# Attention two heads at a time on one core: both key halves of the array in one pair of steps

## The reference, cut to what matters

```python
s = jnp.einsum('bqkgd,bskd->bkgqs', qblk, k).astype(jnp.float32) * scale
pr = jax.nn.softmax(s, axis=-1).astype(v.dtype)
return jnp.einsum('bkgqs,bskd->bqkgd', pr, v)
```

## Time and profile before

| | us |
|---|---|
| median of 3 runs | 3143.61 |
| lowest and highest | 3140.13, 3146.26 |
| the profiled execution | 3126.22 |
| its span | 3124.4 |
| TensorE, VectorE, GpSimd, ScalarE busy | 2777.1, 2225.4, 1640.1, 574.6 |
| attention of group 0, first scores to next matmul | 128.86 to 154.22 |
| attention of group 1 | 299.00 to 372.4 |
| attention of group 2 | 892.65 to 1061.45 |

### The profile page before, as it was taken

The page is one execution under the profiler, slowest core; times in us unless marked ns, Lnnn a source line. Parts: engine busy times, 40 slices in busy tenths (PEclk is TensorE's granted clock), DMA queues, the critical chain, the costliest instruction groups (busy, mean ns, idle before and its releaser), DMA issues.

```text
span 3124.4 us, 34577 instructions
## 1 busy us (share of the span) xinstructions
PE 2777.1 (89%) x9441; PEld 1620.8 (52%) x9441; DVE 2225.4 (71%) x4681; ACT 574.6 (18%) x983; POOL 1640.1 (52%) x1444
## 2 busy tenths in 40 slices
PE   7999998795258876967999999999999999999997
PEld 6785565465134435533366555555555545545553
DVE  1336567999988777899988677777777766655554
ACT  2311502210024200111166311111011111100001
POOL 0001354346577677456832466666666656655451
PEclk9999999898666788988999999999999999999999
DMA  4375698778789899777877899999999999998984
GB/s 148 108 236 176 181 340 285 265 274 299 246 300 310 302 372 370 251 236 249 276 268 270 325 401 403 401 401 399 390 397 389 378 372 401 401 347 323 327 318 167
DMA packets 360703, 961.16 MB, mean 308 GB/s; under 512 B 28065, under 2 KB 152737, under 8 KB 359073
## 3 DMA queue, kind: packets, MB, share of 16 engines
q0 software_dynamic: 184320, 671.17, 58.8%
q1 hardware_dynamic: 175136, 284.69, 26.3%
q10 hardware_dynamic: 1152, 4.19, 0.3%
HBM read 930.58 MB, written 29.36 MB: 307 GB/s over the span
## 4 chain that ended last, share of the span: by engine, by line
PE 67%; DVE 16%; DMA 6%; issue 4%; ACT 4%; POOL 2%; POOLq 0%; ACTq 0%; SPq 0%; DVEq 0%
PE o_bank L766 21%; PE bank L776 21%; PE bank L541 10%; DVE ring L1103 8%; PE bank L712 5%; PE bank L529 5%; DMA ring<-in_expert_u,idx_now 3%; POOL ring L1070 2%; PE o_bank L747 2%; PE bank L519 1%; PE o_bank L621 1%; PE bank L611 1%; DMA wslot<-in_expert_uT 1%; DMA ring<-in_expert_v,idx_now 1%; ACT region_p L970 1%
## 5 line engine op out<-in xcount | busy, mean ns | idle before, releaser
L1070 POOL DMA_INDIRECT ring<-in_expert_u,idx_now x640 | 784.5, 1226 | 461.4 <-DVE dots L1103 230.4
L1070 POOL DMA_INDIRECT ring<-in_expert_v,idx_now x640 | 750.7, 1173 | 467.0 <-issue 148.2
L766 PE MATMUL o_bank<-region_b,wslot 128*128 128x384 f32 x2048 | 687.8, 490 | 13.1 <-DMA wslot<-in_expert_uT 13.1
L776 PE MATMUL bank<-wslot,region_q 128*128 128x512 f32 x1536 | 679.9, 592 | 0.0
L1103 DVE CUSTOM_DVE_ANT_0 ring<-ring,h 128x1024 f32<-128x1024 f32 x512 | 606.2, 1220 | 63.4 <-DMA ring<-in_expert_u,idx_now 55.4
L1411 DVE SCALAR_TENSOR_TENSOR region_c<-ring,dots,region_c 128x1024 f32<-128x1024 f32 x384 | 492.9, 1284 | 105.5 <-DMA ring<-in_expert_v,idx_now 69.7
L766 PEld LDWEIGHTS o_bank<-region_b,wslot 128*128 128x128 f32 x2048 | 392.0, 192 | 315.8 <-issue 64.8
L776 PEld LDWEIGHTS bank<-wslot,region_q 128*128 128x128 f32 x1536 | 291.8, 190 | 340.3 <-issue 306.6
L1062 POOL COPY idx_now<-idx 128x8 uint32 x160 | 104.7, 654 | 509.5 <-DVE idx L1340 293.5
L712 PE MATMUL bank<-ring,region_s 128*128 128x512 f32 x512 | 246.7, 610 | 59.2 <-ACT region_s L948 49.2
L990 ACT ACTIVATE region_q<-o_bank 128x384 f32<-128x384 f32 x128 | 62.9, 491 | 980.6 <-PE o_bank L766 980.6
(11 more groups left out here) (158 smaller groups left out, 2529.3 us busy)
## 6 DMA issues: line engine op xcount, KB each, us to landing
wslot<-in_expert_uT SPq DMA_DIRECT2D x128, 512.0 KB, 11.8
wslot<-in_expert_v SPq DMA_DIRECT2D x128, 512.0 KB, 6.8
wslot<-in_w_in SPq DMA_DIRECT2D x34, 1024.0 KB, 7.0
wslot<-in_w_query SPq DMA_DIRECT2D x24, 1024.0 KB, 8.0
region_p<-expert_weights SPq DMA_DIRECT2D x20, 768.0 KB, 14.9
wslot<-in_w_out SPq DMA_DIRECT2D x12, 1024.0 KB, 11.6
expert_weights<-region_q SPq DMA_DIRECT2D x6, 2048.0 KB, 7.4
expert_weights<-region_p SPq DMA_DIRECT2D x6, 2048.0 KB, 7.4
```

What stands on the lines that cost most here:

```text
L766: ins = nc.tensor.matmul(dense_in[q][:, 0:DENSE_T], u_cols[slot][:, k, :], h2T[:, k, T - DENSE_T:T], start=(k == 0), stop=(k == KD - 1))
L776: ins = nc.tensor.matmul(dense_out[2 * t + n][:], hidden[q][:, t * P:(t + 1) * P], v_cols[slot][:, n * 512:(n + 1) * 512], start=start, st ...
L1070: nc.gpsimd.indirect_dma_start(ring[:, r, :], None, table, bass.IndirectOffsetOnAxis(ap=idx_now[:, half, r:r + 1], axis=0)).then_inc(row_l ...
```

## The change

Steps are taken in pairs (m is steps 2m and 2m+1, the two halves of the same j). TensorE issues both score matmuls of a pair one after the other, turns both steps, and interleaves the value matmuls of the two halves. `probs`, `neg_max` and `prob_sum` get four buffers; the transposes go to four half tiles in `gate_attn` and `keys_sb`, which attention did not use before. VectorE and ScalarE take maxima, exponentials, scalings and copies two at a time. No instruction is added or taken away.

```diff
--- before.py
+++ after.py
@@ -137,12 +137,15 @@
                 yield (gg, "qT", j), None
         yield (g, "kT"), None
     n = len(attention_steps(g))
-    yield (g, "s", 0), None
-    yield (g, "s", 1), None
-    for i in range(n):
+    for i in range(0, n, 2):
+        if i == 0:
+            yield (g, "s", 0), None
+            yield (g, "s", 1), None
         if i + 2 < n:
             yield (g, "s", i + 2), None
+            yield (g, "s", i + 3), None
         yield (g, "probsT", i), None
+        yield (g, "probsT", i + 1), None
     for c in range(KD // 2):
         for d in (2 * c, 2 * c + 1):
             yield (g, "gate_attn", d), (g, "gate_attn", c)
@@ -243,8 +246,8 @@
         dots_now = sb("dots_now", [P, BODY])
         stat = sb("stat", [P, 3, TT])
         head_stat = sb("head_stat", [P, TT, QK_HEADS])
-        neg_max = sb("neg_max", [P, 2])
-        prob_sum = sb("prob_sum", [P, 2])
+        neg_max = sb("neg_max", [P, 4])
+        prob_sum = sb("prob_sum", [P, 4])
         eps = sb("eps", [P, 1])
 
         xa = region_b[:, :].rearrange("p (t d) -> p t d", t=TT)
@@ -278,8 +281,14 @@
         mixedTs = [h2[:, 2:4, :].rearrange("p a d -> p (a d)").rearrange("p (g t) -> p g t", g=GROUPS),
                    region_s[:, 0:GROUPS * T].rearrange("p (g t) -> p g t", g=GROUPS)]
         kTs = [late[:, sizes[1]:sizes[1] + T], region_s[:, 0:T]]
-        probs = region_s[:, T:3 * T].rearrange("p (a s) -> p a s", a=2)
-        probsT = region_s[:, 3 * T:5 * T].rearrange("p (a s) -> p a s", a=2)
+        probs = region_s[:, T:5 * T].rearrange("p (a s) -> p a s", a=4)
+        turned_probs = [gate_attn[:, :, :].rearrange("p a t -> p (a t)"),
+                        keys_sb[:, :, :].rearrange("p a n -> p (a n)")]
+
+        def probsT(i):
+
+            return turned_probs[i // 2 % 2][:, i % 2 * T:(i % 2 + 1) * T]
+
         peer_q = region_s[:, 0:2 * T].rearrange("p (a t) -> p a t", a=2)
         score = region_s[:, 2 * T:6 * T].rearrange("p (a t n) -> p a t n", a=4, t=TT)
 
@@ -600,41 +609,44 @@
                 steps = attention_steps(g)
                 t0 = GROUP_OF[g][1][0]
 
-                def scores(i):
-                    t, j, half = steps[i]
-                    if i == 0:
+                def scores(m):
+                    t, j, _ = steps[2 * m]
+                    if m == 0:
                         moved(pe, FIRST_GROUP[b], "kT")
                         for jj in range(PAIRS):
                             moved(pe, g, "qT", jj)
-                    bank = fill(g, "s", i)
-                    rows = slice(half * HD, (half + 1) * HD)
-                    ins = nc.tensor.matmul(bank[:], qTs[g][rows, j, (t - t0) * P:(t - t0 + 1) * P],
-                                           kTs[b][rows, :], start=True, stop=True)
-                    done(ins, g, "s", i)
-
-                def values(i):
-                    t, j, half = steps[i]
-                    if j == 0 and half == 0 and b * TT + t >= 2:
+                    pair = [fill(g, "s", 2 * m + half) for half in range(KV_HEADS)]
+                    for half in range(KV_HEADS):
+                        rows = slice(half * HD, (half + 1) * HD)
+                        ins = nc.tensor.matmul(pair[half][:], qTs[g][rows, j, (t - t0) * P:(t - t0 + 1) * P],
+                                               kTs[b][rows, :], start=True, stop=True)
+                        done(ins, g, "s", 2 * m + half)
+
+                def values(m):
+                    t, j, _ = steps[2 * m]
+                    if j == 0 and b * TT + t >= 2:
                         pe.wait_ge(o_freed[t % 2], (b * TT + t) // 2)
-                    moved(pe, g, "probsT", i)
+                    for half in range(KV_HEADS):
+                        moved(pe, g, "probsT", 2 * m + half)
                     for s in range(TT):
-                        ins = nc.tensor.matmul(o_banks[t % 2][half * HD:(half + 1) * HD, j, :],
-                                               vs[b][:, s, half * HD:(half + 1) * HD],
-                                               probsT[:, i % 2, s * P:(s + 1) * P],
-                                               start=(s == 0), stop=(s == TT - 1))
-                    if j == PAIRS - 1 and half == 1:
+                        for half in range(KV_HEADS):
+                            ins = nc.tensor.matmul(o_banks[t % 2][half * HD:(half + 1) * HD, j, :],
+                                                   vs[b][:, s, half * HD:(half + 1) * HD],
+                                                   probsT(2 * m + half)[:, s * P:(s + 1) * P],
+                                                   start=(s == 0), stop=(s == TT - 1), skip_group_check=True)
+                    if j == PAIRS - 1:
                         ins.then_inc(o_filled[t % 2], 1)
 
                 scores(0)
-                scores(1)
-                for i in range(len(steps)):
-                    if i + 2 < len(steps):
-                        scores(i + 2)
-                    pe.wait_ge(probs_ready, STEPS_BEFORE[g] + i + 1)
-                    turned((g, "probsT", i), range(TT), lambda s: probs[:, i % 2, s * P:(s + 1) * P])
-                    if i:
-                        values(i - 1)
-                values(len(steps) - 1)
+                for m in range(len(steps) // 2):
+                    if 2 * m + 2 < len(steps):
+                        scores(m + 1)
+                    for i in (2 * m, 2 * m + 1):
+                        pe.wait_ge(probs_ready, STEPS_BEFORE[g] + i + 1)
+                        turned((g, "probsT", i), range(TT), lambda s: probs[:, i % 4, s * P:(s + 1) * P])
+                    if m:
+                        values(m - 1)
+                values(len(steps) // 2 - 1)
 
             for g, (b, tiles) in enumerate(GROUP_OF):
                 if g == FIRST_GROUP[b]:
@@ -882,10 +894,10 @@
                 def exp(i):
                     bank = filled(act, g, "s", i)
                     act.wait_ge(max_ready, before + i + 1)
-                    if i >= 2:
-                        filled(act, g, "probsT", i - 2)
-                    nc.scalar.activation(probs[:, i % 2, :], bank[:], ACT.Exp, bias=neg_max[:, i % 2:i % 2 + 1],
-                                         accum_out=prob_sum[:, i % 2:i % 2 + 1]).then_inc(exp_ready, 1)
+                    if i >= 4:
+                        filled(act, g, "probsT", i - 4)
+                    nc.scalar.activation(probs[:, i % 4, :], bank[:], ACT.Exp, bias=neg_max[:, i % 4:i % 4 + 1],
+                                         accum_out=prob_sum[:, i % 4:i % 4 + 1]).then_inc(exp_ready, 1)
 
                 def outputs(t):
                     act.wait_ge(o_filled[t % 2], (b * TT + t) // 2 + 1)
@@ -893,14 +905,18 @@
                                          ACT.Identity).then_inc(o_freed[t % 2], 1)
 
                 exp(0)
-                for i in range(n):
-                    if i + 1 < n:
-                        exp(i + 1)
-                    if g:
-                        moved(act, g, "s", i)
-                        nc.scalar.activation(probs[:, i % 2, :], probs[:, i % 2, :], ACT.Identity,
-                                             scale=prob_sum[:, i % 2:i % 2 + 1]).then_inc(probs_ready, 1)
-                    move(probsT[:, i % 2, :], (g, "probsT", i))
+                exp(1)
+                for i in range(0, n, 2):
+                    if i + 2 < n:
+                        exp(i + 2)
+                        exp(i + 3)
+                    for ii in (i, i + 1):
+                        if g:
+                            moved(act, g, "s", ii)
+                            nc.scalar.activation(probs[:, ii % 4, :], probs[:, ii % 4, :], ACT.Identity,
+                                                 scale=prob_sum[:, ii % 4:ii % 4 + 1]).then_inc(probs_ready, 1)
+                    for ii in (i, i + 1):
+                        move(probsT(ii), (g, "probsT", ii))
                     if i % HEADS == 0 and i:
                         outputs(GROUP_OF[g][1][i // HEADS - 1])
                 outputs(GROUP_OF[g][1][-1])
@@ -1177,29 +1193,34 @@
 
             def row_max(g, i):
                 bank = filled(dve, g, "s", i)
-                if i >= 2:
-                    dve.wait_ge(exp_ready, STEPS_BEFORE[g] + i - 1)
-                nc.vector.tensor_reduce(neg_max[:, i % 2:i % 2 + 1], bank[:], AX.X, ALU.max,
+                if i >= 4:
+                    dve.wait_ge(exp_ready, STEPS_BEFORE[g] + i - 3)
+                nc.vector.tensor_reduce(neg_max[:, i % 4:i % 4 + 1], bank[:], AX.X, ALU.max,
                                         negate=True).then_inc(max_ready, 1)
 
             def invert_sum(g, i):
                 dve.wait_ge(exp_ready, STEPS_BEFORE[g] + i + 1)
 
-                total = prob_sum[:, i % 2:i % 2 + 1]
+                total = prob_sum[:, i % 4:i % 4 + 1]
                 nc.vector.reciprocal(total, total).then_inc(frees(g, "s", i), 1)
                 if g == 0:
```

(13 more changed lines are left out.)

## The result

The changed kernel takes 3218.4 us (median of 4 runs, 3213.5 to 3221.0), the kernel before 3144.9 beside it: a ratio of 1.0232, with a 95% interval of 1.0211 to 1.0252. It is slower by 73.5 us; the forecast was +81, to 3224 us. The profiled execution took 3220.99 us, with a span of 3218.9.

What follows compares the result with a forecast made beforehand. TensorE was taken to bound group 1, while VectorE's own work is 4.35 of group 2's 5.28 us a step. Terms 0 + 31 + 56 - 6 = +81 us on the 3143.6 us median gave 3224 us, range 3176 to 3264.

Steps and rivals of the forecast that it cites:

- The order closes a loop: Attention: both next-pair maxima precede this pair's reciprocals, leaving no slack, so each pair waits for its scores; 70% with low clock.
- The loop in group 1: Second attention stage, 24 steps: a pair takes 7.3 us at full clock, 9.6 at half, against 5.67; stage +31 us.
- The share of low clock: Second attention stage: TensorE's clock is low for three quarters of the time, making the loop 9.1 us.
- Group 2: Third attention stage, 32 steps, three row products each: loop 14.4 us, stage 225 us against 168.8, +56.
- the tail: End of the third attention stage, after its thirteen loops: forecast at 24 us.
- Group 0: First attention stage, 8 steps without row products: no change, between -4 and +3 us, of 25.4.
- Halves at once: TensorE's array halves work together: a pair of scores costs what one cost, paired values 1.09 us instead of 1.85.
- The credit of 6 us: Behind the third attention stage: a full ring when that stretch starts shortens VectorE's waits for gathered rows, -6 us.
- The sum: Whole kernel: 0 + 31 + 56 - 6 = +81 us, put on the median of 3143.6, gives 3224 us.
- B: Rival, 13%: the loop closes but the clock stays high; about +25 to +45 us, 3178 us.
- C: Rival, 12%: values do not overlap in the array; +81 and some 50 us, 3275 us.
- D: Rival, 3%: faster, TensorE's work decides; second attention stage -22 us, 3121 us.

Runs made afterwards that it cites:

- e1: Changed kernel with both next-pair maxima moved behind this pair's reciprocals and both next-pair exponentials behind the scalings; 3092.0 us, ratio 0.9868 to the kernel before.
- e3: Changed kernel with only ScalarE's order turned round, scalings before the next pair's exponentials; 3196.8 us (one run).
- e9: Changed kernel with idle TensorE matmuls in each loop's gap, written to the bank of the next but one scores; 3176.7 us (one run).
- e5: Changed kernel with a pair's value matmuls not interleaved, all four of one half, then all four of the other; 3236.3 us (one run).
- e10: The e1 version with the value matmuls of a pair not interleaved; 3113.7 us (one run).
- e8: Changed kernel's TensorE pairs, with VectorE and ScalarE one step at a time as before, output bank one step later; 3149.9 us, ratio 1.0006.
- e7: The e1 version with TensorE's part as in the kernel before, one half at a time; 3200.3 us (one run).

## Why the prediction was right

- **The order closes a loop.** Right, by e1 to e3: turn the orders round and 53 and 55 us go. The signs that were named are there: TensorE idles 3.35 us before each first turn, VectorE waits for scores before the first maximum of a pair and not the second, and the granted clock in group 1 is 0.69.
- **The loop in group 1**, 7.3 us at full and 9.6 at half rate. Right: 7.28 in e9 with the clock held, 9.58 where a loop ran wholly at the low level (324.63 to 334.21). The gap was to be 3.4 us and is 3.35.
- **The share of low clock**, three quarters, so 9.1: 9.16 measured. The number was chosen (three quarters of the way from 7.3 to 9.6 would be 9.0), and the stage's 104.4 against 104.1 owes something to luck. Over the nine loops the granted clock was 0.67, so two thirds of the time were low; the loop is as long as forecast because the low part falls on what closes it: turn to values and values to scores are at half rate in nearly every loop, 1.05 and 1.90, while much of the full level falls into the gap (317.13 to 320.47: TensorE idle, granted clock 0.94).
- **Group 2** at +56 was too large; it is +45.9, or +42.7 against the second profile of before. The term is the loop of 14.4 us, where 13.75 were measured: I had the scores at half rate, 2.07 us; in most loops the clock comes back while they run, and they take 1.55 and 1.44 in the rows above. Thirteen loops make 8.5 us of the 10, and the tail the rest: 24 forecast, 21.9 measured (1118.96 to 1140.90).
- **Group 0** at 0: it is -1.2.
- **Halves at once.** Right for the scores: a pair reaches the turn after 1.06 us in e1 (303.14 to 304.20), one score took 1.05. By the rule of strict order that the Trainium skill gives (TensorE: Matmul & The Clock Gate, what overlaps) it would, as an estimate, be some 0.4 us more; the trace disagrees. The values, for which no row stood, overlap fully where they alternate (e5). The 0.8 and 1.9 us for values that do not were too large, 0.5 (e10) and 0.9 (e5): they were read from the row of x16, where the second eight start at 371.33, when ScalarE's copy for them is through.
- **The credit of 6 us** behind group 2 is the term that failed. From the end of group 2 to the first weighted sums the changed kernel takes 360.5 us and before took 366.4, and VectorE's wait for gathered rows in that stretch is 29.4 us against 35.7. That looks like the credit, but the second profile of before has 361.0 and a wait of 29.0, and e1, with no slower attention, 362.9 and 30.4. So it is a difference between executions.
- **The sum** came within 6 us of the median partly by luck: group 2 was 10 us too high and the credit took 6 of it back.
- **Rivals.** B (clock stays high) was a real alternative: e9 is its picture, but without filling matmuls the granted clock was 0.69. C fell with e5, D with the loop; its price for group 1, 22 us, is what e1 measured once the loop was open (50.9 against 73.4).

## What to carry to other kernels

Before giving an engine two steps at a time, write the order of every engine side by side and look for what was issued just before that the next wait needs: an engine's capacity and a deeper buffer help only if a step of slack stays between the request and its use. Here the changed kernel lost 2.3% because both maxima were put ahead of both reciprocals; with them behind, and the exponentials behind the scalings, the same matmuls gain 1.3% over the kernel before, and TensorE is busy for 42.5 us in group 1 instead of 66.0 (e1). A loop with gaps is priced twice, once for its latencies and once for the clock that the gaps cost; in group 1 the second was 17 of 31 us.

## What the runs showed of the hardware that was not expected

- Score matmuls of the two row halves in float32, two records each, ran as two at a time although the code issues them head after head: a pair held the array for 1.06 us against 1.05 for one.
- Value matmuls of the two column halves: 16 records took 1.90 us at the low level where they alternate and 2.81 in turn, 1.02 and 1.51 at the full one.
- In e8's group 1, with a gap of 2.16 us in most loops, the granted clock was 0.78. In e7's, with one wait of 1.1 to 1.6 us in each pair, it was 0.64, though TensorE was busy for 100 of 119 us; in e9's, where it was busy for 70 of 87, it was 0.96.
- Matmuls of no use made the changed kernel faster: e9 adds 132 matmuls whose results nobody reads, and its group 1 is 17 us shorter than the changed kernel's and its group 2 18 us.
